# Gate/up turns of a two-layer trunk: two and a half sets of seven products in place of two, alternating PSUM banks, and an addend accumulated straight from DRAM

## The reference, cut to what matters

```
def swiglu(x, wg, wu, wd):
    return (jax.nn.silu(x @ wg) * (x @ wu)) @ wd
...
h = h + swiglu(rmsnorm(h, ffn_norm[layer]), w_gate[layer], w_up[layer], w_down[layer])
```

## Time and profile before

| | |
|---|---|
| median of 3 runs | 1650.39 us (1650.2 to 1650.5) |
| the profiled execution, first to last instruction (span) | 1649.6 us |
| PE busy | 1639.0 us, 99% |
| DVE busy | 1433.4 us, 87% |
| ACT busy | 1137.2 us, 69% |
| matmuls of the gate/up turns | 20 turns of 180 |
| DMA engines, mean bandwidth | 233 GB/s |

### The profile page before, as it was taken

The page is one execution under the profiler, slowest core; times in us unless marked ns, Lnnn a source line. Parts: engine busy times, 40 slices in busy tenths (PEclk is TensorE's granted clock), DMA queues, the critical chain, the costliest instruction groups (busy, mean ns, idle before and its releaser), DMA issues.

```text
span 1649.6 us, 19819 instructions
## 1 busy us (share of the span) xinstructions
PE 1639.0 (99%) x7456; PEld 1351.4 (82%) x7456; DVE 1433.4 (87%) x1604; ACT 1137.2 (69%) x1596; POOL 128.4 (8%) x164
## 2 busy tenths in 40 slices
PE   9999999999999999999999999999999999999998
PEld 8888888888888888888777888888888888888887
DVE  7889999999999899777676868999999999888867
ACT  6677777777767755556665566777777776676653
POOL 1100000000000000002010000000000000000000
PEclk9999999999999999999999999999999999999999
DMA  8578888888887886845434557888888888887883
GB/s 297 176 216 259 265 258 259 259 260 257 261 258 228 257 268 191 281 177 180 153 128 154 179 182 201 255 257 257 258 259 260 259 260 258 284 241 243 230 255 148
DMA packets 179063, 384.67 MB, mean 233 GB/s; under 512 B 7316, under 2 KB 7444, under 8 KB 178840
## 3 DMA queue, kind: packets, MB, share of 16 engines
q1 hardware_dynamic: 162832, 324.67, 56.6%
q0 software_dynamic: 15840, 57.68, 18.4%
q10 hardware_dynamic: 296, 1.06, 0.2%
HBM read 323.61 MB, written 2.10 MB: 197 GB/s over the span
## 4 chain that ended last, share of the span: by engine, by line
PE 96%; DVE 2%; DMA 1%; SPq 0%; issue 0%; ACT 0%
PE acc L1798 9%; PE acc L1799 9%; PE acc L1800 9%; PE acc L1811 8%; PE acc L1812 8%; PE acc L1813 8%; PE acc L1675 6%; PE acc L1677 6%; PE acc L1676 6%; PE acc L1905 6%; PE acc L1903 6%; PE acc L1904 6%; PE acc L1888 3%; PE acc L1890 3%; PE acc L1889 3%; DMA raw<-pool_w_in 1%
## 5 line engine op out<-in xcount | busy, mean ns | idle before, releaser
L1269 DVE TENSOR_TENSOR w_lo<-raw,w_hi 128x1024 fp32r<-128x1024 f32 x440 | 524.7, 1216 | 36.2 <-ACT w_hi L792 29.9
L792 ACT ACTIVATE w_hi<-raw 128x1024 fp32r<-128x1024 f32 x440 | 459.6, 1059 | 133.6 <-PE acc L1800 77.5
L850 ACT ACTIVATE w_hi<-raw 128x1024 fp32r<-128x1024 f32 x221 | 234.0, 1061 | 158.6 <-PE acc L1905 120.6
L1441 DVE TENSOR_TENSOR w_lo<-raw,w_hi 128x1024 fp32r<-128x1024 f32 x221 | 266.3, 1221 | 58.1 <-ACT w_hi L850 52.3
L1799 PE MATMUL acc<-w_lo,xT_hi 128*128 128x512 f32 x640 | 249.0, 389 | 0.0
L1800 PE MATMUL acc<-w_hi,xT_lo 128*128 128x512 f32 x640 | 249.0, 389 | 0.0
L1798 PE MATMUL acc<-w_hi,xT_hi 128*128 128x512 f32 x640 | 249.0, 389 | 0.0
L1903 PE MATMUL acc<-w_hi,hT_hi 128*128 128x512 f32 x456 | 177.5, 389 | 0.1
L1904 PE MATMUL acc<-w_lo,hT_hi 128*128 128x512 f32 x456 | 177.4, 389 | 0.0
L1905 PE MATMUL acc<-w_hi,hT_lo 128*128 128x512 f32 x456 | 177.4, 389 | 0.0
L1800 PEld LDWEIGHTS acc<-w_hi,xT_lo 128*128 128x128 f32 x640 | 120.1, 188 | 25.0
(11 more groups left out here) (204 smaller groups left out, 2802.0 us busy)
## 6 DMA issues: line engine op xcount, KB each, us to landing
raw<-w_gate_in SPq DMA_DIRECT2D x88, 1024.0 KB, 7.3
raw<-w_up_in SPq DMA_DIRECT2D x88, 1024.0 KB, 5.3
raw<-w_down_in SPq DMA_DIRECT2D x88, 1024.0 KB, 6.9
raw<-raw POOLq DMA_DIRECT2D x110, 512.0 KB, 5.3
raw<-w_q_in SPq DMA_DIRECT2D x16, 1024.0 KB, 5.1
raw<-w_o_in SPq DMA_DIRECT2D x16, 1024.0 KB, 5.1
raw<-w_kv_in SPq DMA_DIRECT2D x4, 1024.0 KB, 6.7
raw<-pool_w_in SPq DMA_DIRECT2D x3, 1024.0 KB, 13.9
```

Source lines behind the costliest of these rows:

```text
L792: nc.scalar.activation(w_hi[:, (before + n) % RING, :], raw[:, slot, off:off + 2 * C], ACT.Copy).then_inc(hi_ready, 1)
L1269: nc.vector.tensor_tensor(w_lo[:, w, :], weight_half(unit), w_hi[:, w, :].bitcast(F32), ALU.subtract).then_inc(unit_ready, 1)
L1441: nc.vector.tensor_tensor(w_lo[:, LAP_DOWN[l].ring(n), :], src, w_hi[:, LAP_DOWN[l].ring(n), :].bitcast(F32), ALU.subtract).then_inc(unit_ ...
```

## The change

- **A half set.** Row tiles 8 and 9, one tile in each half of the inner dimension, get the seven products too (set 2, `HALF_SET`). `("gate", 4)` and `("up", 4)` go. In come `HB` (B11 and B21 side by side, 1024 columns), `HU` (T2 and T4, 1024 columns) and `HT1`, `HB22`, `HT3` of 512 columns each: 21 matmuls for the 24 of the two units that go. A turn has 25 units and 177 matmuls. The five activation rows of the half set (`row_hi`, `row_lo`, `minus_hi`, `minus_lo`) are made once per layer in the first block (`act_half_sums`), and they take the tenth half slot of `raw`.
- **Combination in PSUM.** The family shares two banks: B11, T2 and T3 one, T1 and B22 the other; ACT copies the running sum out four times a turn (`chain_copy`: first, fifth, second, third), each copy a wait of PE for the next form. The signs of B11 and of some rows are turned, so that gate and up then each need one DVE add of 128x1024 (`gate_add`, `up_add`) in place of the six steps before. Odd turns use PSUM banks 4 to 7, even turns banks 0 to 3.
- **Addend from DRAM.** B12 isn't loaded any more. Six accumulating DMAs a turn add it from DRAM onto B11 (giving T1) and B22 (giving T3).
- **Layout and loads.** The host stores `w_gate` and `w_up` block by block, so that runs of 4 KB are read. SP loads 512 KB pieces into nine half slots, in an order planned ahead (`TurnsPlan`): 14 a turn.

```diff
-SUM_SETS = 2
+SUM_SETS = 3
+HALF_SET = 2
+SUM_ORDER = [("B11", 1), ("HB", 2), ("B11", 0), ("gate", 6), ("gate", 7), ("T1", 1), ("HT1", 2),
+             ("T1", 0), ("gate", 5), ("B22", 1), ("B22", 0), ("B21", 1), ("HU", 2), ("T2", 0),
+             ("HB22", 2), ("T2", 1), ("B21", 0), ("T4", 1), ("T3", 1), ("T3", 0), ("HT3", 2),
+             ("T4", 0), ("up", 5), ("up", 6), ("up", 7)]
...
+ACCUM_ORDER = [("T1", 1), ("HT1", 2), ("T1", 0), ("T3", 1), ("T3", 0), ("HT3", 2)]
+CHAIN = {"first": ("B11", "HB"), "fifth": ("T1", "HT1"), "second": ("T2", "HU"), "third": ("T3", "HT3")}
...
+NEEDS = {"T2": "first", "HU": "first", "B22": "fifth", "HB22": "fifth", "T3": "second", "HT3": "second", "up": "third"}
...
+            def chain_copy(l, j, step, dst, bank, scale=1.0):
+
+                ac.wait_ge(unit_used, sum_units(l, j) + AT[LINK[step]] + 1)
+                nc.scalar.activation(dst, acc[:, bank, :], ACT.Copy, scale=scale).then_inc(chain_copied, 1)
...
+                    if n == 6:
+                        ac.wait_ge(quad_full, turned + 1)
+                        chain_copy(l, j, "first", act[:, 0, :], up1, -1.0)
+                        if j < NFB - 1:
+                            for part in (0, 1, 2, 3):
+                                quad_move(l, j - 1, part)
...
+                    if n == 23:
+                        ac.wait_ge(quad_full, turned + 2)
+                        chain_copy(l, j, "third", act[:, 1, :], up1, -1.0)
...
+                    if unit[0] == "B11":
+                        nc.vector.scalar_tensor_tensor(out=lo, in0=src, scalar=-1.0, in1=hi, op0=ALU.mult,
+                                                       op1=ALU.subtract).then_inc(unit_ready, 1)
...
+                    if n == 2:
+                        if j > 1:
+                            up_add(l, j - 1)
+                        if j > 1:
+                            common_out(l, j - 1)
...
+                        gp.dma_start(raw_half(j, form, s), b12, accum_op=ALU.add).then_inc(landed[s], 16)
```

More of the change, by code:

```diff
@@ L82 @@
 SUM_STEPS = SUM_UNITS * SUM_TURNS
[L85 to L98, removed]
@@ L101, in turn_half @@
[L101 to L111, removed]
-SLOTS = RING + 1
+T_SUMS = {("T2", 2): 6, ("T2", 1): 6, ("T4", 2): 7, ("T2", 0): 9, ("T4", 1): 14, ("T4", 0): 18}
@@ new lines @@
+GATE_LAST = max(AT[u] for u in SUM_ORDER if u[0] in ("gate", "T4", "HU", "B21"))
+SLOTS = RING + 1
+HALVES = 2 * SLOTS - 1
+PLACE = {"B11": "B11", "T1": "B11", "T2": "B11", "B21": "B21", "T4": "B21", "B22": "B22", "T3": "B22",
+         "gate": "gate", "up": "up", "HB": "HB", "HT1": "HB", "HU": "HB", "HB22": "HB22", "HT3": "HB22"}
+PARTS = {"HB": ("B11", "B21"), "HT1": ("T1",), "HB22": ("B22",), "HU": ("T2", "T4"), "HT3": ("T3",)}
+@dataclass
+class Piece:
+    half: int
+    nth: int
+    ready: int
+    first: int
+    turn: int
+    form: str
+    n: int
@@ new lines, with __init__ @@
+class TurnsPlan:
+    def __init__(self):
+        life = {}
+        for unit in SUM_ORDER:
+            life.setdefault((PLACE[unit[0]], unit[1]), []).append(AT[unit])
+        for s in range(SUM_SETS):
+            whole = ("B11", s) in life
+            life["B11" if whole else "HB", s].append(T_SUMS["T4", s] + 1)
+            life["B22" if whole else "HB22", s].append(T_SUMS["T2", s])
+        self.free = [n + 1 - UD for n in range(2 * RING)] + [-2 * UD] * (HALVES - 2 * RING)
+        self.count = [0] * HALVES
+        self.of, self.pieces = {}, []
+        for j in range(1, NFB):
+            for key in sorted(life, key=lambda key: min(life[key])):
+                half = min(range(HALVES), key=lambda one: (self.free[one], one))
+                self.count[half] += 1
+                start = SUM_UNITS * (j - 1)
+                piece = Piece(half, self.count[half], self.free[half], start + min(life[key]), j, *key)
+                self.free[half] = start + max(life[key]) + 1
+                self.of[j, *key] = piece
+                self.pieces.append(piece)
+        self.pieces.sort(key=lambda one: (one.ready, one.first))
@@ L600, in _ @@
             load_gate_up(0, 0)
[L601 to L602 removed]
+            load_sum_turns(0)
             load_down(0)
@@ L1810, in sum_turn @@
-                        dst = banks[form]
-                        nc.tensor.matmul(dst, x_hi, w_hi[:, w, cols], start=starts[0] and kk == 0, stop=False)
-                        nc.tensor.matmul(dst, x_hi, w_lo[:, w, cols], start=False, stop=False)
-                        last = nc.tensor.matmul(dst, x_lo, w_hi[:, w, cols], start=False, stop=stops[0] and kk == 1)
+                                tok, bank = slice(t * P, (t + 1) * P), touched(unit)[t]
+                                dst, start, stop = acc[:, bank, :], starts[bank] and kk == 0, stops[bank] and kk == 1
@@ new lines, in sum_turn @@
+                        bank = banks[part]
+                        dst, start = acc[:, bank, :], starts[bank] and (halved or kk == 0)
+                        stop = stops[bank] and (halved or kk == 1)
+                        nc.tensor.matmul(dst, x_hi, w_hi[:, w, cols], start=start, stop=False, skip_group_check=True)
+                        nc.tensor.matmul(dst, x_hi, w_lo[:, w, cols], start=False, stop=False, skip_group_check=True)
+                        last = nc.tensor.matmul(dst, x_lo, w_hi[:, w, cols], start=False, stop=stop, skip_group_check=True)
```

396 lines of the change are left out of this document (225 added, 171 removed).

## The result

The changed kernel takes 1668.6 us (median of 4 runs, 1663.2 to 1669.7) against 1650.5 for the kernel before on the same chip: ratio 1.0099, 95% interval 1.0087 to 1.0111. It is 1.0% slower. I had forecast 1641.4, and a range that ended at 1652.

The account below looks back on a forecast made before the run. PE's matmul count was taken as the bound: of 0.68 us a turn won (13.6 in all), 0.23 is lost to order, leaving 20 x 0.45 = 9.0 us, so 1650.4 - 9.0 = 1641.4; range 1636.5 to 1652.

Parts of the forecast that it names:

- Matmuls, 13.6 us: On PE, 177 matmuls a turn in place of 180 take 13.6 us off; a turn would last 40.12.
- DVE and ACT in sum, 38.6 and 35.5 of 40.12: Work per turn after the change: DVE 38.6 us and ACT about 35.5 of 40.12, so ACT's order decides.
- Accumulates, "Cost: nothing": The DRAM accumulates for T1 and T3 land in about 6 us, before ACT needs them, costing nothing.
- limits of 7.8 and 6.9: Landing times up to which the accumulates of T1 (set 1) and HT1 cost ACT nothing: 7.8 and 6.9 us.
- rival D: HT1's accumulate lands late, holding ACT's queue at unit 6; slower than before, 1677 us; chance 0.18.
- D's formula: For HT1 landing beyond 7.35 us: 20 turns times lateness past 6.9 less 0.45; 27 us at 8.7.
- Losses by order, 0.23 a turn: PE waits for late low parts: 0.07 at unit 3, 0.02 at unit 8, about 0.14 at unit 19.
- My allowance of 0.15: A low part on DVE must end about 0.15 us before its matmul is due on PE.
- rival C: Stalls from dearer 512-column operations on DVE and ACT eat the gain: turns of 40.7 to 40.9, 1646 to 1652; chance 0.17.
- Down's first load: Head of the down stage: load asked for 4 us later than before, at most 0.5 us per layer, taken as nothing.
- Transfers in sum, and 512 KB pieces: DMA work per turn is 32 us against 33, no new bound; the smaller loads' start is hidden, costing nothing.
- the 80 us: Loss if the fixed 2.0 us or so of six more load transfers a turn were not hidden.

Follow-up runs that it names:

- one weight sum less: The kernel with the three edits, without DVE's T4 weight sum of the first set: 1638.8 us, ratio 0.9927 to the kernel before.
- The best version: The second order with the first set's T2 sum behind unit 9 again and the last up tile's load held until unit 17: 1642.1 us, ratio 0.9948.
- the longer hold: Changed kernel with two loads (third gate tile, first set's B22) asked for only after the first gate tile's low part: 1651.0 us, ratio 1.0000.
- the second order: The kernel with the three edits, with ACT's moves and fifth copy and DVE's weight sums reordered: 1658.0 us, ratio 1.0042.
- without accumulates: Changed kernel without the three accumulates a turn that make T1 and their waits: 1650.9 us, ratio 0.9997 to the kernel before.
- the three edits: Changed kernel with the longer hold, DVE's order moved at units 3 and 8, and `gate_add` behind down's first low part: 1646.0 us, ratio 0.9968.

## Why the prediction was wrong, step by step

- **Matmuls, 13.6 us: right.** 7396 instructions, and turns of 40.12 where nothing binds (one weight sum less): 12.2 us faster than before, with 1.3 lost at the head of down.
- **DVE and ACT in sum, 38.6 and 35.5 of 40.12: right to within 0.7.** The best version shows 38.86 and 34.66 in 40 us, at turns of 40.21. The half high parts take 0.63 and the copies 0.58, against my 0.60.
- **Accumulates, "Cost: nothing": the step that failed.** I took 6 us, "since the loads of the next turn are nearly in by then". They were not. Nine loads, asked for from 10 us before the first accumulate to 1.4 us before it, are 4.5 MB; at the 388 GB/s of the earlier trace rows that is 11.5 us of all engines, to 293 at the earliest, 1.2 us after the first accumulate was asked for. Laid out in time, the rate that I had in hand would have said that the accumulates meet them; the last of the nine landed at 301. T1 and HT1 took 9.3 and 8.2 us in the turn shown, 8.9 and 7.9 in the median of the twenty, where I had limits of 7.8 and 6.9. The mechanism was rival D, to which I gave 0.18; it named HT1 and not T1, which ACT waits for longer. From the change to the longer hold the landing's worth is 18 us. At HT1's 8.2, D's formula gives 20 x (8.2 - 7.35) = 17 us over before, against 18 measured, but that it comes so near is luck: it has 20 x (8.2 - 6.9) = 26 for the landing, and nothing for the 8 that order and down cost beyond my forecast.
- **Losses by order, 0.23 a turn: the mechanism was right, the size was half.** Measured without the late landing: 0.13 at unit 3 (0.07 forecast), none at unit 8 (0.02), 0.36 at unit 19 (0.14); none before unit 22, as forecast. PE at unit 19 in the longer hold, in a turn that starts at 335.73:

```profile
364.16 0.39 PE L1925 MATMUL acc<-w_hi,s_lo 128*128 128x512 f32 x1
364.63 0.50 PE L1923 MATMUL acc<-w_hi,s_hi 128*128 128x512 f32 x1
364.96 0.39 PE L1924 MATMUL acc<-w_lo,s_hi 128*128 128x512 f32 x1
```

  The first start is 0.24 late, the next one follows after 0.33, not 0.227, and over the unit PE loses another 0.12 before it is back at its pace. My allowance of 0.15 behind a low part's end held for this, since it was read over the same two steps: between the starts of the earlier trace rows stands this one, 0.22 late, and the next comes 0.34 after it, not 0.227.

```profile
631.55 0.50 PE L1888 MATMUL acc<-w_hi,hT_hi 128*128 128x512 f32 x1
```

  What was mis-sized is when DVE gets there. Unit 19's low part starts at 363.36, 27.63 after the turn's start, where I had 27.41, because DVE waits longer for ACT ahead of it, at units 14 and 16:

```profile
355.64 0.69 DVE L1369 TENSOR_TENSOR w_lo<-raw,w_hi 128x512 fp32r<-128x512 f32 x1 [0.15 <-ACT w_hi L846]
...
358.80 3.50 DVE L1369 TENSOR_TENSOR w_lo<-raw,w_hi 128x1024 fp32r<-128x1024 f32 x3 [0.20 <-ACT w_hi L846]
```

  That is 19.91 and 23.07 after the start, against 19.74 and 22.85 laid out; the second difference, 0.22, goes on whole to unit 19. It is the idling that the second order took away. The gaps between PE's starts without accumulates sum to 9.1 us over all twenty turns, 4.5 more than 20 x 0.23 (the first turns lose 0.4 each, the tenth, without moves on ACT, 0.2 or less). Turns of 40.62 are just under rival C's size (40.7 to 40.9), by another cause than the 512-column rows that I had blamed there: those kept near their price.
- **Down's first load, "at most 0.5 us per layer, taken as nothing": wrong.** It cost 1.7 a layer, 3.5 in all. I had counted the lateness of the load and not the queue behind it: `gate_add`, the SiLU and three high parts. For the first layer the three edits show that; in the second 1.4 is still lost with that order mended, and why is not shown.
- **Transfers in sum, and 512 KB pieces: right.** In 292 to 295 the pieces move 1.08 MB in 3 us, 360 GB/s at a share of 1.02, against 388 at 1.05 for 1 MB loads. The Trainium skill's rule to batch to 1 MiB or more ("DMA: Bandwidth & Descriptors", section Bandwidth) does not show here: in the changed kernel ACT waits for no load of gate or up (its waits for `w_up_in` are for accumulates). The fixed 2.0 us that I took from its section Anatomy of one DMA is stated there for transfers that GpSimd issues, and these loads are SP's, so the 80 us that I worked out from it rested on a figure for other transfers. Its turn-taking between queues by packets (same page, Queues, rings and completion order) fits 295 to 298, where both queues move at 64% and 42%; why the first packet of the accumulate came some 2.1 us later than in the longer hold, it does not tell.

Put together: 1641.4 forecast, 18 for the landing, 4.5 for the order and 3.5 for down are 1667.4; measured 1668.6. The landing's share is known from two experiments, the order's from gaps in the trace and from turns with and without their cause, and down's is read from gaps in the trace; the 1.2 us that are left are not accounted for.

## What to carry to other kernels

Before a transfer's landing is priced from a median, lay out what its queue's neighbours have asked for in the 10 us before it, in bytes over the rate of a row: here what was outstanding came first, and a load asked for just behind an accumulate cost it 2.2 us too. An accumulate that gates an engine in mid-turn is protected by holding loads that are not urgent, which took three lines of the plan here and gave back all that the change had lost. And a late operand on PE cost its lateness and some 0.12 us more, so that several small losses, each priced at 0.14 or less, can eat a gain of three matmuls.

## What was not expected of the hardware

- Accumulates with a source in DRAM are no slower than those with a source in SBUF: a packet of 4 KB takes 328 ns (median) in the turns of the changed kernel, from DRAM, and as long outside them, from `raw`; the median landing is 5.6 us with the loads held longer, against 4.8 and 6.9 before.
- While loads filled all 16 engines (101.7% in 292 to 295), an accumulate asked for behind them moved its first packet 3.7 us after its issue (median), against 1.6 with the loads held longer.
- A 256 KB accumulate took 4.7 us with the next 512 KB load asked for 3.2 us behind it, and 6.9 with that load asked for 0.9 us behind it.
- After a start that was 0.24 us late PE's first interval was 0.33 us in place of 0.227, at a granted clock that stayed full; the kernel before shows about the same (0.34, from 631.55 to 631.89), where the start was 0.22 late.
